# Stick-breaking attention of one encoder step on one core: from 36 tile rounds to 20 steps of 1024 score columns

## What is computed

```
def sb_attend(q, k, v, q_pos, k_pos):
    z = jnp.einsum('bqhd,bkhd->bhqk', q.astype(f32), k.astype(f32)) * SB_DIM ** -0.5
    mask = k_pos[None, :] < q_pos[:, None]
    log_1mb = jnp.where(mask, jax.nn.log_sigmoid(-z), 0.0)
    after = lax.cumsum(log_1mb, axis=3, reverse=True) - log_1mb
    att = jnp.where(mask, jnp.exp(jax.nn.log_sigmoid(z) + after), 0.0)
    return jnp.einsum('bhqk,bkhd->bqhd', att, v.astype(f32)).astype(v.dtype)

for i0 in range(0, T, Q_BLOCK):        # 8 query tiles of 128; 8 heads of 64
    outs.append(sb_attend(q[:, i0:i1], k[:, :i1], v[:, :i1], ...))
```

## Time and profile before

| | us |
|---|---|
| median of 3 runs | 1826.61 |
| lowest and highest run | 1822.06 and 1827.38 |
| span of the profiled execution | 1821.2 |
| PE busy in that span | 1779.1 (98%) |
| attention stage, from the first scores (131.07) to the last sum (313.38) | 182.3 |
| the same, PE idle in it | 7.7 |

### The profile page before, as it was taken

One profiled execution on the slowest core, in us unless ns is written; L12 is line 12 of the kernel. 1 busy time (PEld: TensorE's weight loads), 2 busy tenths in 40 slices (PEclk: granted clock), 3 DMA queues, 4 the chain that ended last, 5 costly groups with the idle time before them and its releaser, 6 DMA issues.

```text
span 1821.2 us, 25830 instructions
## 1 busy us (share of the span) xinstructions
PE 1779.1 (98%) x10456; PEld 1574.0 (86%) x10456; DVE 1047.8 (58%) x1293; ACT 866.2 (48%) x1124; POOL 130.8 (7%) x142
## 2 busy tenths in 40 slices
PE   8999999999999999999999999989999999999996
PEld 7888887989898899999999988878888888888874
DVE  5336664433355432142333155678889998988965
ACT  4225554332454331121122133257888878788863
POOL 0010000000000010000000000010000110000044
PEclk9999999999999999999999999989999999999998
DMA  5231111102022122122222152189999999999995
GB/s 190 82 107 41 30 31 32 41 24 74 24 67 85 49 74 87 60 86 70 76 83 62 34 187 82 53 307 398 419 411 413 412 412 422 415 411 417 413 374 187
DMA packets 141194, 329.87 MB, mean 181 GB/s; under 512 B 15418, under 2 KB 93078, under 8 KB 116373
## 3 DMA queue, kind: packets, MB, share of 16 engines
q1 hardware_dynamic: 123700, 272.69, 40.3%
q0 software_dynamic: 12624, 38.74, 5.8%
q10 hardware_dynamic: 4752, 16.78, 2.3%
HBM read 292.37 MB, written 39.87 MB: 182 GB/s over the span
## 4 chain that ended last, share of the span: by engine, by line
PE 61%; DVE 1%; DMA 1%; DVEq 1%; issue 0%; ACT 0%; POOL 0%; POOLq 0%; ACTq 0%
PE banks L70 7%; PE banks L71 7%; PE banks L72 7%; PE banks L2132 6%; PE banks L2134 6%; PE banks L2133 6%; PE banks L2158 3%; PE banks L2160 3%; PE banks L2159 3%; PE banks L2011 2%; PE banks L2013 2%; PE banks L2012 2%; PE banks L2118 2%; PE banks L2142 1%; PE banks L2041 1%; PE banks L2026 0%
## 5 line engine op out<-in xcount | busy, mean ns | idle before, releaser
L2615 DVE TENSOR_TENSOR low<-raw,hig 128x2048 fp32r<-128x2048 f32 x192 | 431.6, 2286 | 58.3 <-ACT hig L2318 57.0
L2318 ACT ACTIVATE hig<-raw 128x2048 fp32r<-128x2048 f32 x192 | 359.5, 1916 | 27.2 <-ACT ye L2391 14.4
L2132 PE MATMUL banks<-hig,xel 128*128 128x512 f32 x512 | 202.9, 396 | 0.5 <-DVE xel L2687 0.5
L2134 PE MATMUL banks<-hig,xeh 128*128 128x512 f32 x512 | 200.2, 391 | 0.0
L2133 PE MATMUL banks<-low,xeh 128*128 128x512 f32 x512 | 199.7, 390 | 0.0
L70 PE MATMUL banks<-xhi,glo 128*128 128x384 f32 (+1 forms) x552 | 180.3, 327 | 1.9 <-PEq L65 1.9
L72 PE MATMUL banks<-xhi,ghi 128*128 128x384 f32 (+1 forms) x552 | 180.4, 327 | 0.0
L71 PE MATMUL banks<-xlo,ghi 128*128 128x384 f32 (+1 forms) x552 | 180.2, 327 | 0.0
L70 PE MATMUL gproj<-xhi,glo 128*128 128x384 f32 (+1 forms) x384 | 130.3, 339 | 0.0
L72 PE MATMUL gproj<-xhi,ghi 128*128 128x384 f32 (+1 forms) x384 | 125.6, 327 | 0.0
L71 PE MATMUL gproj<-xlo,ghi 128*128 128x384 f32 (+1 forms) x384 | 125.5, 327 | 0.0
(11 more groups left out here) (461 smaller groups left out, 3622.8 us busy)
## 6 DMA issues: line engine op xcount, KB each, us to landing
raw<-in_w_e_gate_dram SPq DMA_DIRECT2D x64, 1024.0 KB, 7.9
raw<-in_w_e_up_dram SPq DMA_DIRECT2D x64, 1024.0 KB, 8.2
raw<-in_w_e_down_dram SPq DMA_DIRECT2D x64, 1024.0 KB, 7.4
graw<-in_w_in_dram SPq DMA_DIRECT2D x39, 512.0 KB, 3.9
expert_rows<-ye ACTq DMA_DIRECT2D x31, 512.0 KB, 8.3
xt<-in_x_prompt_dram SPq DMA_DIRECT2D x16, 512.0 KB, 3.6
expert_rows<-nil POOLq DMA_DIRECT2D x16, 512.0 KB, 4.0
braw<-in_w_branch_dram SPq DMA_DIRECT2D x24, 256.0 KB, 2.9
```

The lines of the kernel that those rows point to most:

```text
L2132: nc.tensor.matmul(bank[:, :], xel[n % 2][:, kk, :], wh[:, k, :], start=(kk == 0), stop=False)
L2134: last = nc.tensor.matmul(bank[:, :], xeh[n % 2][:, kk, :], wh[:, k, :], start=False, stop=(kk == KC - 1))
L2318: nc.scalar.activation(hig[q % HI][:, :], raw[q % RAW][:, :], ACT.Copy).then_inc(high, 1)
L2615: nc.vector.tensor_tensor(low[q % RAW][:, :], raw[q % RAW][:, :], hig[q % HI][:, :].bitcast(F32), ALU.subtract).then_inc(lowed, 1)
```

## The change

A pair now has 5 steps in place of 9 rounds: `[(7,), (6, 0), (3, "d"), (5, 1), (4, 2)]`. Each but the third has exactly 1024 score columns for each head. Two tiles of a step share the bank pair `zz`, are turned into sigmoids by one instruction a head (1024 columns; in the third step 1024 and 576), and are scanned apart. Every step has four fills, held in four buffers `attT` (three before); 20 fills a pair.

The stagger is one step. TensorE's order in step t is: turn fills 0 and 1 of step t-1, scores of t, average fills 0 and 1, projections, turn fills 2 and 3, average fills 2 and 3. A projection is cut into quarters of 6 products, which `slots` deals out to the steps; pair 1 and 2 have a cache turn in step 0, a whole projection in steps 1 and 2, and one spread over steps 3 and 4. Pair 3 has half a projection in steps 1 to 4 and a whole one behind the last step. `wrq` has a second place for blocks 1 and up, which is loaded once the block before is split. The first weights of pair 1 are split in step 0.

```
-    wrq = at("wrq", [P, KC, P], F32, R2 + 8192)
+    wrq = [at("wrq", [P, KC, P], F32, off) for off in (R2 + 8192, R2 + 32768)]
-    attT = [at("attT", [P, 512], F32, SUF0 + 10240 + 2048 * i) for i in range(3)]
+    attT = [at("attT", [P, 512], F32, SUF0 + off) for off in (4096, 10240, 12288, 14336)]
-    ORDER = ["d", 7, 0, 6, 1, 5, 2, 4, 3]
-    QSTEP = [[3, 5, 6]] + [[1, 3, 5]] * (HW - 1)
-    CSTEP, SSTEP, LAG = 7, 8, 2
...
+    STEPS = [(7,), (6, 0), (3, "d"), (5, 1), (4, 2)]
+    sfx = [at("sfx", [P, 2048], F32, ATT0 + 8192 * i) for i in range(2)]
+    fills = [[b[0:2], b[2:4], b[4:5], b[5:6]] if has_d(t) else [b[i:i + 2] for i in range(0, 8, 2)] for t, b in enumerate(blocks)]
+    NF = 4
+    slots = [(part(0, 1, 0, 2), part(0, 1, 2, 4)), ([], part(1, 0, 0, 2)), (part(1, 0, 2, 4), []),
+             (part(1, 1, 0, 2), part(1, 1, 2, 4)), (part(1, 2, 0, 2), part(1, 2, 2, 4))]
+    for hp in range(1, HW - 1):
+        b = hp + 1
+        slots += [([], [("c", hp, 0, 0)]), (part(b, 0, 0, 2), part(b, 0, 2, 4)), (part(b, 1, 0, 2), part(b, 1, 2, 4)),
+                  (part(b, 2, 0, 1), part(b, 2, 1, 2)), (part(b, 2, 2, 3), part(b, 2, 3, 4))]
+    slots += [([], [("c", HW - 1, 0, 0)]), (part(HW, 0, 0, 1), part(HW, 0, 1, 2)), (part(HW, 0, 2, 3), part(HW, 0, 3, 4)),
+              (part(HW, 1, 0, 1), part(HW, 1, 1, 2)), (part(HW, 1, 2, 3), part(HW, 1, 3, 4)), (part(HW, 2, 0, 3), part(HW, 2, 3, 4))]
...
             def q_load(b):
-                sp.wait_ge(qprod, 3 * b)
-                sp.dma_start(wrq[:, :, :], w_in_k[:, :, c0:c0 + P]).then_inc(wq_in, 16)
+                sp.wait_ge(qwl, b)
+                sp.dma_start(wrq[1][:, :, :], w_in_k[:, :, c0:c0 + P]).then_inc(wq_in, 16)
...
-            for t in range(NR + LAG):
...
+            for t in range(NR + 1):
+                hp, i = t // NS, t % NS
+                if t:
+                    turn(t - 1, 0)
+                    turn(t - 1, 1)
                 if t < NR:
...
                     score(t)
+                before, amid = slots[t]
+                if t:
+                    average(t - 1, 0)
+                    average(t - 1, 1)
+                between_turns(before)
+                between_turns(amid)
+                if t:
+                    turn(t - 1, 2)
+                    turn(t - 1, 3)
+                    average(t - 1, 2)
+                    average(t - 1, 3)
...
             def rest(t):
+                for u in range(2):
+                    act.wait_ge(scored, 2 * t + u + 1)
+                    if t >= 2:
+                        act.wait_ge(tfilled, NF * (t - 1))
+                    z0, o, w = (448, 1024, 576) if has_d(t) and u else (0, 1024 * u, 1024)
+                    nc.scalar.activation(sfx[t % 2][:, o:o + w], zz[u][:, z0:z0 + w], ACT.Sigmoid, scale=-1.0).then_inc(sdone, 1)
...
+            for t in range(NR + 1):
+                hp, i = t // NS, t % NS
+                if t:
+                    evacuate(t - 1, 0)
+                    evacuate(t - 1, 1)
                 if t < NR:
                     rest(t)
+                before, amid = slots[t]
+                high(before)
+                high(amid)
+                if t == 0:
                     q_split(1)
+                if t:
+                    evacuate(t - 1, 2)
+                    evacuate(t - 1, 3)
+                if i == NS - 1 and hp + 2 <= HW or t == NR:
                     q_split(hp + 2 if t < NR else HW + 1)
...
+            for t in range(NR + 2):
+                hp, i = t // NS, t % NS
+                if t >= 2:
+                    collect(t - 2)
+                before, amid = slots[t] if t <= NR else ([], [])
+                if t < NR:
+                    scan(t, 0)
+                low(before)
+                if t < NR:
+                    scan(t, 1)
+                low(amid)
```

More of the change, by code:

```diff
@@ new lines, in build, with key0 @@
+    NS = len(STEPS)
+    DSTEP = STEPS.index((3, "d"))
+    steps = [(hp, xs) for hp in range(HW) for xs in STEPS]
+    NR = len(steps)
+    has_d = lambda t: "d" in steps[t][1]
+    nblk = lambda x: x + 1
+    sfx = [at("sfx", [P, 2048], F32, ATT0 + 8192 * i) for i in range(2)]
+    scans = [3 if "d" in xs else 2 * len(xs) for _, xs in steps]
+    scans_upto = lambda t: sum(scans[:t + 1])
+    def key0(t, x, u):
+        xs = steps[t][1]
+        if "d" in xs:
+            return 512 if x == "d" else 1088 * u
+        return 1024 * u + (nblk(xs[0]) * P if x != xs[0] else 0)
@@ new lines, in build, with part @@
+    blocks = [[(x, j) for x in xs for j in (range(nblk(x)) if x != "d" else ["cache", "own"])] for _, xs in steps]
+    fills = [[b[0:2], b[2:4], b[4:5], b[5:6]] if has_d(t) else [b[i:i + 2] for i in range(0, 8, 2)] for t, b in enumerate(blocks)]
+    NF = 4
+    def part(b, g, q0, q1):
+        return [("q", b, g, q) for q in range(q0, q1)]
+    slots = [(part(0, 1, 0, 2), part(0, 1, 2, 4)), ([], part(1, 0, 0, 2)), (part(1, 0, 2, 4), []),
+             (part(1, 1, 0, 2), part(1, 1, 2, 4)), (part(1, 2, 0, 2), part(1, 2, 2, 4))]
@@ L200, in build, with extent @@
         half = lambda t, i: t[:, 512 * i:512 * i + 512]
[L202 to L205, removed]
-            return P, 256 * min(2, x + 1 - 2 * i)
+        def extent(t, i):
+            return (DEC, P) if has_d(t) and i == 3 else (P, 512)
         OBK, PQ = half(mix, 0), half(mix, 1)
@@ L443, in score @@
-                if x == "d":
-                    o, w = sp2[-1]
-                    nc.tensor.matmul(zz[0][:, o + w - DEC:o + w], identb[:, :], neverd[:, :],
-                                     start=False, stop=True, skip_group_check=True).then_inc(scored, 1)
-            def turn(t, f):
-                hp, x = rounds[t]
-                bank = half(tb, f % 2)
-                i = fill[t].index(f)
+                    for c in range(2):
+                        out = zz[0][:, 512:1024] if c == 0 else zz[1][:, 448:512]
+                        for i in range(3):
+                            q = (qbl, qbh, qbh)[i][:, :]
+                            k = (ckTh, ckTl, ckTh)[i][:, :] if c == 0 else (kTh, kTl, kTh)[i][:, hp, SEQ:T]
+                            product = nc.tensor.matmul(out, q, k, start=(i == 0), stop=(i == 2 and c == 0), skip_group_check=True)
+                        if c == 0:
+                            product.then_inc(scored, 1)
@@ L511, in _ @@
                 else:
-                    query(0, 2)
+                    for q in range(4):
+                        query(0, 2, q)
                     turn_cache(0)
@@ L515, in _ @@
                 turn_k(t)
-            query(0, 0)
+            for q in range(4):
+                query(0, 0, q)
             pe.wait_ge(masks, 1)
@@ L769, in _, with low @@
+                last.then_inc(ocopied, 1)
+            def low(slot):
+                for kind, b, g in ends(slot):
+                    if kind == "q":
+                        q_low(b, g)
+                    else:
+                        c_low(b)
             ve.wait_ge(const, 1)
```

301 lines of the change are left out of this document (126 added, 175 removed).

## The result

The changed kernel took 1838.2 us (median of 6 runs, 1833.88 to 1844.94), the kernel before 1825.69 (6 runs, 1821.13 to 1827.95). The ratio is 1.0077, with an interval of 1.0054 to 1.0099: slower by about 0.8%. The profiled execution took 1835.58 us with a span of 1833.9.

What follows compares the result with a forecast made beforehand. TensorE was taken as the bound. Added idle +9.6 (copy and scan waits), work -2.4, GpSimd +2.1 and stage end +1.6 gave +10.9 us on 1826.61: 1837.5 us, range 1829 to 1844.

Runs made afterwards that it cites:

- e8: The kernel before, with two VectorE subtractions whose result nobody reads added behind the last sum of the attention; 1828.8 us, one run.
- e1: The changed kernel, with the running product of each step's second head made over only 8 columns of each tile; 1826.45 us, ratio 1.0001.
- e7: The changed kernel's steps and fills reordered: scores two steps ahead of their turns, work between turns and averages; 1832.17 us, ratio 1.0038.
- e9: e7 with one line moved: SyncE loads the next raw weights ahead of its wait for the sample rows' averages; 1815.85 us, ratio 0.9944.
- e3: The changed kernel, with the next weights split one step earlier and the last pair's projections placed as in pairs 1 and 2; 1839.9 us, ratio 1.0083.
- e4: The changed kernel, with 16 transposes whose result nobody reads added on TensorE behind the last average; 1833.2 us, ratio 1.0061.
- e10: The changed kernel word for word, run and profiled again; 1840.1 us, ratio 1.0083.
- e5: The changed kernel, with GpSimd's subtraction of the cached values cut to 8 of its 512 columns; 1835.6 us, one run.

## What to carry to other kernels

Count a stagger in microseconds: what is ready when, against what the consumer does meanwhile. Fewer rounds do not make the scans shorter (4.47 us a step for two scans of 1024 columns, 4.57 for the same columns in four scans), and a stagger of one step of 9.5 us (47.7 by five) did not hide 5.65 us of sigmoid and scan, since much of the step lay on the wrong side of the scores. Where work is to cover waits, put it between a producer and its consumer on the waiting engine, once for each such pair, and look which loads it drags along on their queue: a good order lost its whole gain, about 18 us of stage, to one load issued behind the wrong wait. An engine left idle where a barrier stands costs more than the idle itself if its clock falls behind it.

## What was not expected of the hardware

TensorE's clock after idle time was not told by the length of that idle alone. At the change of stage: 1.52 us idle, no fall; 3.10 and 3.14, half speed from the first product on (e8, changed kernel); in e1 also 3.14, but there the first product took 0.41, and the slow ones (0.53) began 1.6 us later, at 314.39. 1.8 us idle, no fall in e7 and e9, a fall in e3; the last three waits ahead of it were 0.57, 0.57 and 0.25 in e3 and 0.25 each in e7 and e9, and no run tests whether that is the reason. Inside the stage: 1.24 us with a fall in e3, 2.07 at 137.61 without one in e4 and 2.29 at 137.89 without one in e10, and the same waits of the changed kernel with and without. A fall in the stage cost about 1.5 us behind waits of 1.2 to 2.3, and 2.7 behind waits of over 3 (e7). At the change of stage the products stood 0.32 apart for 3.1 us in the changed kernel (324.58 to 327.7) and for 5.6 in e8 (315.23 to 320.8), which is why the same idle cost 1.45 in one and 2.6 in the other. It is not the order that decides: e5, with the changed kernel's order, also had slow products for 5.6 us (323.94 to 329.52) and lost 2.6.

The GpSimd instruction can grow beside scans too, but not each time. The one of 8 columns a partition (e5) took 0.27 us with no scan beside it, and 0.92, 0.20 and 0.50 beside scans. The one of 512 columns took 1.30 mostly ahead of the scans (131.54) and 1.30 to 1.72 beside them in the changed kernel, up to 2.31 in e10 (at 220.00).
